# Who makes the low parts of the second and third super-block's operands: DVE or POOL

## The chip, the cores and the metric

The kernel runs on one core of one Trainium2 chip. The metric is the device time of one launch in microseconds. TensorE is called PE, VectorE DVE, ScalarE ACT, GpSimd POOL and SyncE SP.

## The reference

One layer of a streaming encoder with a width of 1024 runs over 2096 columns (2064 of a new stream and 32 of a running one). The mixer comes first, the SwiGLU feed-forward part second:

```python
xp = xp + mp                                   # mixer
xp = xp + _swiglu(_rmsnorm(xp, norm2_g[l]), w_gu[l], w_down[l])

def _swiglu(xn, w_gu, w_down):                 # w_gu 1024 x 5632, w_down 2816 x 1024
    gu = xn @ w_gu
    g, u = jnp.split(gu, [D_FF], axis=-1)
    return (jax.nn.silu(g) * u) @ w_down
```

A final RMSNorm gives the outputs. Everything is float32.

## The kernel before

**Precision.** Each float32 operand of a matmul is split in two fp32r tiles: a high part, which ACT writes as a copy, and a low part, the operand less its high part. Three matmuls (high by high, high by low, low by high) give one product. This is done to weights and to activations alike. DVE makes the low parts of the weights (`split_lo`, L1590), ACT their high parts (`split_hi`, L795), in a ring of three slots (`wring`).

**Feed-forward part.** The columns stand in three super-blocks s = 0, 1, 2 of 2 x 348, 2 x 346 and 2 x 346 columns. The two halves of a super-block and the two halves of the contraction and of the output make a 2 x 2 by 2 x 2 matrix product, which is done with seven products in place of eight. For each of four contraction tiles j the seven operands are four tiles as they are, and three differences with a fourth made of them. They stand in `ycomb[:, combination, high or low, j, :]`. A super-block runs through gate/up steps 0 to 10 (`gate_up`) and down groups 0 to 5 (`down`), in the order gu0, gu1, gu2, dn0, gu3, gu4, dn1, ... gu9, gu10, dn4, dn5. Each step and group uses seven weight slots. A slot is 24 matmuls in dn4 and 12 in dn5, where the group has one pair of tiles instead of two. Down products land in PSUM, and DVE adds them to `xacc` (`add_down`, L1579), 14 additions a group.

**The operand of the next super-block** is made while dn4 and dn5 run, by three engines:

- POOL, `operand(s, j)` (L550 to L561), for j = 0 to 3. It issues three DMAs that load four tiles of `ys` into `work`, waits for them, makes the differences of 692 columns (L557) and of 346 (L559 and L561). Loads of j = 2 and 3 first wait for the low parts of j - 2, the differences of j for the low parts of j - 1. POOL starts when DVE has made the last low part of gate/up step 10.
- ACT, `operand_hi(s, j)` (L1004 to L1009): four copies, the first two once the loads have landed, the third after L559, the fourth after L561. They are placed in ACT's list in group dn4 before the weight splits of slots 2, 3, 5 and 6 (`REBUILD`), each split being that for three slots later.
- DVE, `operand_lo(s, j)` (L1465 to L1471): four subtractions of 692, 346, 1038 and 346 columns, each after ACT's matching copy, placed in DVE's list in group dn4 after the additions of slots 2, 3, 5 and 6.

Each engine's list is in order, so a wait in it holds all that follows. PE's first matmul of the next super-block waits for all 16 high and 16 low increments:

```python
if p == k == 0:
    pe.wait_ge(a_hi, 16 * (s + 1))
    pe.wait_ge(a_lo, 16 * (s + 1))
```

The operand of super-block 0 is made in the mixer's last block by the same functions, at other places (`BUILD`, `TAKE`).

Of the kernel before, what the change touches and what calls it, by code (L numbers as in the profile page):

```python
# [31 lines left out]
NT = 3  # L32
TH = (348, 346, 346)
# [134 lines left out]
REBUILD = {2: 0, 3: 1, 5: 2, 6: 3}  # L168
# [64 lines left out]
def build(nc, dx, dwm, dws, dcst, dfix, dst0, graw, draw, dy, dst, fused, sgu, sdn, x1s, ys):  # L233
    f32 = mybir.dt.float32
# [3 lines left out]
    MUL, ADD, SUB = ALU.mult, ALU.add, ALU.subtract  # L238
    base = -(-nc.sbuf_base // 64) * 64
    ctx = ExitStack()  # L240
    with ctx:
        def sem(name):
            return ctx.enter_context(nc.semaphore(name))

        def at(offset, name, shape, dt=f32):
            return nc.alloc_sbuf_tensor_at(name, shape, dt, offset=base + offset)
# [10 lines left out]
        work = at(e0, "work", [P, 15, HW])  # L257
# [8 lines left out]
        ycomb = at(a0, "ycomb", [P, 7, 2, 4, HW], f32r)  # L266
# [22 lines left out]
        y_made, y_in, y_diff, a_hi, a_lo = sem("y_made"), [sem("y_in0"), sem("y_in1")], sem("y_diff"), sem("a_hi"), sem("a_lo")  # L289
# [95 lines left out]
        def after_gu(s, what, i):  # L385

            n = STEPS.index((what, i))
            return n > 0 and STEPS[n - 1][0] == "gu"
# [5 lines left out]
        def y_base(j):  # L394

            return 7 + 4 * (j % 2)
# [76 lines left out]
        def _(pool):  # L473
# [67 lines left out]
            def load_acc(s):  # L541
                for m in range(KT):
                    pool.dma_start(xacc[:, m, 0:2 * TH[s]], x1s[m, :, TO[s]:TO[s] + 2 * TH[s]]).then_inc(x1_in, 16)

            def operand(s, j):

                n, w, b0 = 4 * s + j, TH[s], y_base(j)
                if j >= 2:
                    pool.wait_ge(a_lo, 4 * (n - 1))
                pool.dma_start(work[:, b0:b0 + 2, 0:w],  # L550
                               ys[j, :, TO[s]:TO[s] + 2 * w].rearrange("p (t c) -> p t c", t=2)).then_inc(y_in[j % 2], 16)
                pool.dma_start(work[:, b0 + 2, 0:w], ys[j + 4, :, TO[s] + w:TO[s] + 2 * w]).then_inc(y_in[j % 2], 16)
                pool.dma_start(work[:, b0 + 3, 0:w], ys[j + 4, :, TO[s]:TO[s] + w]).then_inc(y_in[j % 2], 16)
                pool.wait_ge(y_in[j % 2], 48 * (n // 2 + 1))
                if j:
                    pool.wait_ge(a_lo, 4 * n)
                nc.gpsimd.tensor_tensor(work[:, 3:5, 0:w], work[:, b0 + 1:b0 + 3, 0:w], work[:, b0:b0 + 2, 0:w], SUB).then_inc(y_diff, 1)  # L557
                pool.wait_ge(y_diff, 3 * n + 1)
                nc.gpsimd.tensor_tensor(work[:, 5, 0:w], work[:, b0 + 2, 0:w], work[:, 3, 0:w], SUB).then_inc(y_diff, 1)  # L559
                pool.wait_ge(y_diff, 3 * n + 2)  # L560
                nc.gpsimd.tensor_tensor(work[:, 6, 0:w], work[:, b0 + 3, 0:w], work[:, 5, 0:w], SUB).then_inc(y_diff, 1)  # L561

            pool.wait_ge(tables_in, 32)
            for b in range(NB):
                chunks = prep_range(b)
# [35 lines left out]
            for s in range(NT - 1):  # L601
                pool.wait_ge(h_lo, 4 * PAIRS * (s + 1))
                pool.wait_ge(y_kept, 16 * KT * NB)
                for j in range(4):
                    operand(s + 1, j)
                for n, m in enumerate(NORM_ORDER):
                    pool.wait_ge(y_done, 8 * s + n + 1)
                    pool.dma_start(dy[m, :, TO[s]:TO[s] + 2 * TH[s]], xacc[:, m, 0:2 * TH[s]]).then_inc(y_stored, 16)
                pool.wait_ge(y_stored, 16 * KT * (s + 1))
                load_acc(s + 1)  # L610
# [609 lines left out]
        def _(dve):  # L1220
# [241 lines left out]
            def operand_lo(s, j):  # L1462
                n, w, b0 = 4 * s + j, TH[s], y_base(j)
                dve.wait_ge(a_hi, 4 * n + 1)
                V.tensor_tensor(ycomb[:, 0:2, 1, j, 0:w], work[:, b0:b0 + 3:2, 0:w], ycomb[:, 0:2, 0, j, 0:w].bitcast(f32), SUB).then_inc(a_lo, 1)  # L1465
                dve.wait_ge(a_hi, 4 * n + 2)
                V.tensor_tensor(ycomb[:, 5, 1, j, 0:w], work[:, b0 + 3, 0:w], ycomb[:, 5, 0, j, 0:w].bitcast(f32), SUB).then_inc(a_lo, 1)
                dve.wait_ge(a_hi, 4 * n + 3)
                V.tensor_tensor(ycomb[:, 2:5, 1, j, 0:w], work[:, 3:6, 0:w], ycomb[:, 2:5, 0, j, 0:w].bitcast(f32), SUB).then_inc(a_lo, 1)
                dve.wait_ge(a_hi, 4 * n + 4)  # L1470
                V.tensor_tensor(ycomb[:, 6, 1, j, 0:w], work[:, 6, 0:w], ycomb[:, 6, 0, j, 0:w].bitcast(f32), SUB).then_inc(a_lo, 1)  # L1471

            def norm_sum(s, i):
                n, w = KT * s + i, 2 * TH[s]
                dve.wait_ge(n_sq, n + 1)
                if i == 0:
                    V.tensor_copy(ntot[:, 0:w], nsq[:, n % 2, 0:w]).then_inc(n_sum, 1)
                else:
                    dve.wait_ge(n_sum, n)
                    V.tensor_tensor(ntot[:, 0:w], ntot[:, 0:w], nsq[:, n % 2, 0:w], ADD).then_inc(n_sum, 1)  # L1480
# [100 lines left out]
            def split_lo(n):  # L1581
                if n >= NS:
                    return
                dve.wait_ge(w_hi, n + 1)
                name, c = SLOTS[n], slot_width(n)
                if name[0] == "w":
                    V.scalar_tensor_tensor(wring[:, n % RING, 1, :], wraw[:, n % RAW, :], cst[:, PSC, name[2]:name[2] + 1],
                                           wring[:, n % RING, 0, :].bitcast(f32), MUL, SUB).then_inc(w_lo, 1)
                else:
                    V.tensor_tensor(wring[:, n % RING, 1, 0:c], wraw[:, n % RAW, 0:c], wring[:, n % RING, 0, 0:c].bitcast(f32), SUB).then_inc(w_lo, 1)  # L1590
# [136 lines left out]
            for s in range(NT):  # L1727
                for what, i in STEPS:
                    if what == "gu":
                        gate_up(s, i)  # L1730
                        continue
                    for hh in range(14):
                        if hh % 2 == 0 and (hh or not after_gu(s, "dn", i)):
                            split_lo(SLOT[("dn", s, i, hh // 2)] + RING - 1)
                        add_down(s, i, hh)
                        if hh % 2 and s < NT - 1 and i == 4 and hh // 2 in REBUILD:
                            operand_lo(s + 1, REBUILD[hh // 2])
                        if hh % 2 and s == NT - 1 and i == 5 and hh >= 9:
                            norm_sum(s, hh // 2 - 4)
            for i in range(3, KT):  # L1740
# [79 lines left out]
```

## Time and profile before

| what | value |
|---|---|
| time, median of 3 runs | 2899.11 us (2894.8 to 2900.23) |
| the profiled execution | 2899.26 us, span 2897.4 us |
| PE busy | 2720.9 us (94%) |
| DVE busy | 2104.6 us (73%) |
| ACT busy | 1367.3 us (47%) |
| POOL busy | 250.6 us (9%) |
| mean granted clock of TensorE | 0.981 |

The span is what the trace covers, the execution's own time is a little longer. Busy shares are averages over stages with different limits. The rows below are in microseconds from the start of the span, unless marked ns; what stands in square brackets is how long the engine idled before the instruction, and what ended that.

### The profile page before, as it was taken

The numbers are of one execution on the slowest core, as the hardware profiler recorded it, in microseconds if no ns is written. First come the engines' busy times: TensorE is split into PE (matmuls) and PEld (weight loads), VectorE is DVE, ScalarE is ACT, GpSimd is POOL, SyncE is SP. The second block draws the span as 40 slices with busy tenths as digits, with TensorE's granted clock in tenths as the row PEclk, the third lists the DMA queues.
The fourth block names the chain that finished last, engine by engine and source line by source line (L and its number), as shares of the span: only waits on it lengthen the run. The fifth ranks groups of instructions, "written<-read, shape, count | busy, mean of one in ns | idle before, by whom it ended". The sixth has DMA issues, their size and how long they took to land.

```text
span 2897.4 us, 39533 instructions
## 1 busy us (share of the span) xinstructions
PE 2720.9 (94%) x15404; PEld 2676.2 (92%) x15404; DVE 2104.6 (73%) x2784; ACT 1367.3 (47%) x1849; POOL 250.6 (9%) x425
## 2 busy tenths in 40 slices
PE   8999999999999999999799999889999979999995
PEld 6999999999999999999799999789999979899995
DVE  6867788688868877876676566787666677666667
ACT  6743583366447544833444343454344435334442
POOL 2000101020110011021300000300000030000000
PEclk9999999999999999999899999999999999999998
DMA  6353567456655855574543443445343434534442
GB/s 225 125 180 122 187 224 265 150 202 240 212 184 184 280 190 174 201 260 139 178 154 131 133 128 127 130 142 197 125 131 131 133 129 143 190 124 131 131 131 87
DMA packets 166729, 481.87 MB, mean 166 GB/s; under 512 B 18800, under 2 KB 41840, under 8 KB 166544
## 3 DMA queue, kind: packets, MB, share of 16 engines
q1 hardware_dynamic: 124368, 345.21, 35.7%
q0 software_dynamic: 31664, 117.66, 11.8%
q10 hardware_dynamic: 10512, 16.46, 2.0%
q8 instruction: 124, 2.03, 0.3%
q14 instruction: 61, 0.50, 0.1%
HBM read 414.75 MB, written 64.51 MB: 165 GB/s over the span
## 4 chain that ended last, share of the span: by engine, by line
PE 67%; DVE 15%; ACT 7%; issue 5%; DMA 2%; POOL 2%; SPq 0%; DVEq 0%; ACTq 0%; POOLq 0%
PE ps L635 67%; DVE wring L1590 2%; ACT wring L795 2%; DVE xacc L1579 1%; DMA work<-ys 1%; DVE tmp L1336 1%; DVE work L1545 1%; DVE gb L1305 1%; DVE tmp L1439 1%; POOL work L557 1%; ACT work L1056 1%; DVE main L1721 1%; DVE tmp L1252 1%; DVE xlo L1256 1%; ACT L896 1%
## 5 line engine op out<-in xcount | busy, mean ns | idle before, releaser
L1590 DVE TENSOR_TENSOR wring<-wraw,wring 128x1024 fp32r<-128x1024 f32 (+1 forms) x637 | 768.1, 1206 | 298.8 <-ACT wring L795 296.6
L795 ACT ACTIVATE wring<-wraw 128x1024 fp32r<-128x1024 f32 (+1 forms) x637 | 661.6, 1039 | 620.1 <-PE ps L635 616.6
L635 PE MATMUL ps<-ycomb,wring 128*128 128x346 f32 (+1 forms) x5544 | 890.7, 322 | 23.3 <-issue 14.0
L635 PEld LDWEIGHTS ps<-ycomb,wring 128*128 128x128 f32 x5544 | 887.3, 190 | 25.0 <-issue 25.0
L635 PE MATMUL ps<-xhi,wring 128*128 128x416 f32 (+1 forms) x2560 | 707.7, 354 | 32.9 <-DVE wring L1590 27.6
L635 PE MATMUL ps<-hcomb,wring 128*128 128x346 f32 (+1 forms) x2772 | 477.2, 333 | 90.9 <-DVE xacc L1579 65.8
L635 PEld LDWEIGHTS ps<-hcomb,wring 128*128 128x128 f32 x2772 | 461.3, 197 | 104.8 <-issue 82.4
L635 PEld LDWEIGHTS ps<-xhi,wring 128*128 128x128 f32 x2560 | 482.3, 188 | 47.3 <-DVE wring L1590 26.4
L635 PE MATMUL ps<-xlo,wring 128*128 128x416 f32 (+1 forms) x1280 | 451.5, 353 | 0.0
L635 PE MATMUL ps<-yhi,wring 128*128 128x416 f32 x1280 | 347.1, 351 | 2.6 <-DVE wring L1590 2.6
L1579 DVE TENSOR_TENSOR xacc<-ps,xacc 128x692 f32<-128x692 f32 (+1 forms) x252 | 218.3, 877 | 94.4 <-PE ps L635 90.8
L635 PEld LDWEIGHTS ps<-xlo,wring 128*128 128x128 f32 x1280 | 241.3, 189 | 3.9
L635 PEld LDWEIGHTS ps<-yhi,wring 128*128 128x128 f32 x1280 | 240.2, 188 | 4.8 <-DVE wring L1590 3.2
L635 PE MATMUL ps<-ylo,wring 128*128 128x416 f32 x640 | 224.5, 351 | 0.0
L635 PE MATMUL ps<-mhi,wring 128*128 128x416 f32 x640 | 173.0, 350 | 0.0
L1503 DVE TENSOR_TENSOR work<-ps,work 128x692 f32<-128x692 f32 (+1 forms) x99 | 87.1, 880 | 105.0 <-PE ps L635 105.0
L1015 ACT ACTIVATE work<-ps 128x692 f32<-128x692 f32 (+1 forms) x99 | 74.2, 749 | 177.1 <-PE ps L635 177.0
L635 PEld LDWEIGHTS ps<-ylo,wring 128*128 128x128 f32 x640 | 120.0, 188 | 1.4
L635 PEld LDWEIGHTS ps<-mhi,wring 128*128 128x128 f32 x640 | 120.0, 188 | 0.2
L635 PE MATMUL ps<-mlo,wring 128*128 128x416 f32 x320 | 111.8, 350 | 0.0
L1305 DVE SCALAR_TENSOR_TENSOR gb<-tbuf,cst,gb 128x416 f32<-128x416 f32 (+3 forms) x144 | 80.3, 581 | 20.7 <-ACT gb L864 12.8
L1056 ACT ACTIVATE work<-work 128x1038 f32<-128x1038 f32 (+1 forms) x33 | 35.4, 1074 | 114.9 <-DVE work L1503 114.9
(209 smaller groups left out, 2231.7 us busy)
## 6 DMA issues: line engine op xcount, KB each, us to landing
wraw<-dwm SPq DMA_DIRECT2D x247, 512.0 KB, 3.5
wraw<-sgu SPq DMA_DIRECT2D x132, 512.0 KB, 3.2
wraw<-graw SPq DMA_DIRECT2D x99, 512.0 KB, 3.4
wraw<-sdn SPq DMA_DIRECT2D x120, 256.0 KB, 2.8
wraw<-draw SPq DMA_DIRECT2D x90, 256.0 KB, 2.9
pbuf<-graw POOLq DMA_DIRECT2D x22, 1024.0 KB, 6.9
sgu<-pbuf POOLq DMA_DIRECT2D x22, 1024.0 KB, 6.2
wraw<-fused SPq DMA_DIRECT2D x40, 512.0 KB, 3.3
```

What stands on the lines that cost most here:

```text
L557: nc.gpsimd.tensor_tensor(work[:, 3:5, 0:w], work[:, b0 + 1:b0 + 3, 0:w], work[:, b0:b0 + 2, 0:w], SUB).then_inc(y_diff, 1)
L635: mm = nc.tensor.matmul(out, wt[:, c * P:(c + 1) * P], x, start=(first and q == 0), stop=(last and q == 2), skip_group_check=chain)
L795: A(wring[:, n % RING, 0, 0:c], wraw[:, n % RAW, 0:c], ACT.Copy, scale=cst[:, PSC, name[2]:name[2] + 1] if name[0] == "w" else 1.0).then_i ...
L896: A(tmp[:, 4 * j + 2, 0:bw], tmp[:, 4 * j, 0:bw], ACT.Exp, scale=lac[:, 0, h:h + 1]).then_inc(a_done, 1)
L1015: A(work[:, first:first + 8:7, 0:TH[s]], both(name, TH[s]), ACT.Copy).then_inc(cleared[BANK[name] // 2], 1)
L1056: A(work[:, 0:3, 0:w], work[:, 0:3, 0:w], ACT.Silu).then_inc(silu3, 1)
L1252: V.tensor_tensor(tmp[:, 4 + k % 2, 0:LW], xring[:, k % XR, :], rstd[1][:, 0:LW], MUL).then_inc(xr_done, 1)
L1256: V.scalar_tensor_tensor(xlo[:, m, 0:LW], tmp[:, 4 + m % 2, 0:LW], cst[:, G1, m:m + 1], xhi[:, m, 0:LW].bitcast(f32), MUL, SUB).then_inc(x ...
L1305: V.scalar_tensor_tensor(gb[:, h, c:c + n], t[:, o + v:o + v + n], cst[:, CW0 + v, h:h + 1], gb[:, h, c:c + n], MUL, ADD).then_inc(tap, 1)
L1503: V.tensor_tensor(c, both(name, TH[s]), c, ADD).then_inc(cleared[BANK[name] // 2], 1)
L1579: V.tensor_tensor(out, both(name, w), out, ADD).then_inc(cleared[BANK[name] // 2], 1)
L1590: V.tensor_tensor(wring[:, n % RING, 1, 0:c], wraw[:, n % RAW, 0:c], wring[:, n % RING, 0, 0:c].bitcast(f32), SUB).then_inc(w_lo, 1)
```

## The change

POOL gets a function `operand_rest(s, j)` with the same four subtractions and waits as `operand_lo`, and calls it directly behind `operand(s + 1, j)` for super-blocks 1 and 2. DVE's calls in the down groups go. DVE's `operand_lo(0, ...)` for super-block 0 stays.

```diff
+            def operand_rest(s, j):
+                n, w, b0 = 4 * s + j, TH[s], y_base(j)
+                pool.wait_ge(a_hi, 4 * n + 1)
+                nc.gpsimd.tensor_tensor(ycomb[:, 0:2, 1, j, 0:w], work[:, b0:b0 + 3:2, 0:w], ycomb[:, 0:2, 0, j, 0:w].bitcast(f32), SUB).then_inc(a_lo, 1)
+                pool.wait_ge(a_hi, 4 * n + 2)
+                nc.gpsimd.tensor_tensor(ycomb[:, 5, 1, j, 0:w], work[:, b0 + 3, 0:w], ycomb[:, 5, 0, j, 0:w].bitcast(f32), SUB).then_inc(a_lo, 1)
+                pool.wait_ge(a_hi, 4 * n + 3)
+                nc.gpsimd.tensor_tensor(ycomb[:, 2:5, 1, j, 0:w], work[:, 3:6, 0:w], ycomb[:, 2:5, 0, j, 0:w].bitcast(f32), SUB).then_inc(a_lo, 1)
+                pool.wait_ge(a_hi, 4 * n + 4)
+                nc.gpsimd.tensor_tensor(ycomb[:, 6, 1, j, 0:w], work[:, 6, 0:w], ycomb[:, 6, 0, j, 0:w].bitcast(f32), SUB).then_inc(a_lo, 1)
...
                 for j in range(4):
                     operand(s + 1, j)
+                    operand_rest(s + 1, j)
...
                         add_down(s, i, hh)
-                        if hh % 2 and s < NT - 1 and i == 4 and hh // 2 in REBUILD:
-                            operand_lo(s + 1, REBUILD[hh // 2])
```

## Rows read from the trace of the kernel before

**Rows 1.** The page's first line.

```profile
span 2897.4 us, 39533 instructions
```

**Rows 2.** Stretch, length, PE, PEld, DVE, ACT, POOL busy (count), granted clock, DMA share, GB/s.

```profile
1845.91:1902.02 56.11, 41.62 (x229) 39.30 (x229) 46.10 (x56) 19.78 (x28) 24.30 (x24) 0.91 0.43 139
2336.02:2392.56 56.54, 43.23 (x229) 41.12 (x230) 45.87 (x56) 19.86 (x28) 24.16 (x24) 0.88 0.43 138
```

**Rows 3.** Waits, 1820 to 1890 us: engine, line, released by: total, times, longest.

```profile
PE ps L635 <- DVE xacc L1579: 14.6, 6, 5.0
...
ACT ycomb L1007 <- POOL work L559: 8.6, 4, 2.9
```

**Rows 4.** POOL in order of time, first stretch, and one row of the second.

```profile
1845.91 0.73 POOL L550 DMA_DIRECT2D work<-ys  x1 [365.62 <-DVE hcomb L1565]
...
1847.29 0.54 POOL L553 DMA_DIRECT2D work<-ys  x1
1850.97 1.69 POOL L557 TENSOR_TENSOR work<-work 128x692 f32<-128x692 f32 x1 [3.15 <-DMA work<-ys]
1852.75 1.79 POOL L559 TENSOR_TENSOR work<-work 128x346 f32<-128x346 f32 x1
1854.62 0.94 POOL L561 TENSOR_TENSOR work<-work 128x346 f32<-128x346 f32 x1
1855.49 0.73 POOL L550 DMA_DIRECT2D work<-ys  x1
...
1877.95 1.98 POOL L557 TENSOR_TENSOR work<-work 128x692 f32<-128x692 f32 x1 [2.90 <-DMA work<-ys]
1880.01 1.97 POOL L559 TENSOR_TENSOR work<-work 128x346 f32<-128x346 f32 x1
...
2370.88 1.53 POOL L559 TENSOR_TENSOR work<-work 128x346 f32<-128x346 f32 x1
```

**Rows 5.** PE in order of time, first stretch, and one row of the second.

```profile
1886.32 5.56 PE L635 MATMUL ps<-hcomb,wring 128*128 128x348 f32 x24 [5.00 <-DVE xacc L1579]
1892.43 4.41 PE L635 MATMUL ps<-hcomb,wring 128*128 128x348 f32 x24 [0.55 <-DVE xacc L1579]
...
1902.02 26.80 PE L635 MATMUL ps<-ycomb,wring 128*128 128x346 f32 x168
...
2392.56 26.82 PE L635 MATMUL ps<-ycomb,wring 128*128 128x346 f32 x168
```

**Rows 6.** DVE's groups, 1845.9 to 1902 us: count, busy us, mean ns, idle before.

```profile
L1469 DVE TENSOR_TENSOR ycomb<-work,ycomb 128x1038 fp32r<-128x1038 f32 x4 | 4.9, 1236 | 2.7 <-ACT ycomb L1007 2.7
...
L1465 DVE TENSOR_TENSOR ycomb<-work,ycomb 128x692 fp32r<-128x692 f32 x4 | 4.4, 1093 | 0.2 <-ACT ycomb L1004 0.2
L1467 DVE TENSOR_TENSOR ycomb<-work,ycomb 128x346 fp32r<-128x346 f32 x4 | 2.8, 698 | 0.0
L1471 DVE TENSOR_TENSOR ycomb<-work,ycomb 128x346 fp32r<-128x346 f32 x4 | 2.1, 513 | 0.0
```

**Rows 7.** POOL's groups of differences, 1840 to 1890 us.

```profile
L557 POOL TENSOR_TENSOR work<-work 128x692 f32<-128x692 f32 x4 | 7.2, 1796 | 12.0 <-DMA work<-ys 12.0
L559 POOL TENSOR_TENSOR work<-work 128x346 f32<-128x346 f32 x4 | 6.1, 1534 | 0.3
L561 POOL TENSOR_TENSOR work<-work 128x346 f32<-128x346 f32 x4 | 3.9, 968 | 0.3
```

**Rows 8.** Two weight splits in DVE's order of time.

```profile
1851.71 2.04 DVE L1590 TENSOR_TENSOR wring<-wraw,wring 128x1024 fp32r<-128x1024 f32 x1 [0.27 <-ACT wring L795]
...
1858.22 1.21 DVE L1590 TENSOR_TENSOR wring<-wraw,wring 128x1024 fp32r<-128x1024 f32 x1
```

**Rows 9.** ACT in order of time, behind the fourth operand's third copy.

```profile
1883.00 0.49 ACT L1009 ACTIVATE ycomb<-work 128x346 fp32r<-128x346 f32 x1
1883.40 1.13 ACT L795 ACTIVATE wring<-wraw 128x512 fp32r<-128x512 f32 x2
```

**Rows 10.** Busy time and granted clock as PE comes back.

```profile
1886.00:1888.00 2.00, 1.69 (x6) 1.72 (x7) 1.56 (x3) 0.00 (x0) 0.00 (x0) 0.50 0.41 131
```

## The prediction

> **What bounds the kernel now.** I read the span first: 2897.4 us [rows 1], with 1.86 us outside it in the profiled execution's own 2899.26 us. The code then says where the changed work runs: between the last low part of gate/up step 10 (the DVE increment that opens POOL's operand work) and the first matmul of the next super-block. It happens twice, so I asked for the busy time of each engine in those two stretches [rows 2]. They are 56.11 and 56.54 us long; PE is busy in 41.62 and 43.23 us of them and POOL in 24.30 and 24.16 us. The reader is to see that neither is full: here something waits on something in turn, and a share of busy time says nothing of what ends the stretch.
>
> The waits of the first stretch [rows 3] show PE held by DVE's additions to xacc for 14.6 us, and ACT held by POOL's second difference (L559) for 8.6 us. These belong together. DVE is late because the operand's low part stands ahead of the next addition in its list and waits for ACT's high part; ACT is late because its high part waits for POOL's differences, and the next weight split stands behind it. So I followed POOL in order of time [rows 4]. One operand is a strictly serial turn: three DMA issues from 1845.91 to 1847.83, the wait for their landing until 1850.97, three differences until 1855.56, and at 1855.49 the next operand's issues. POOL never loads ahead, since the loads stand behind the differences of the operand before. Four turns bring the fourth operand's L559 to its end at 1880.01 + 1.97 = 1881.98, 36.07 us after the start. In the second stretch it ends at 2370.88 + 1.53 = 2372.41 [rows 4], 36.39 us after 2336.02 [rows 2]. From there to the next super-block's first matmul it takes 1902.02 - 1881.98 = 20.04 us and 2392.56 - 2372.41 = 20.15 us [rows 4, 5]. That is the sum to be changed: 36.1 + 20.0 = 56.1 us.
>
> **The change, part by part.** It *removes* four low-part subtractions per operand from DVE, four operands in each of two stretches. In the first stretch the four groups take 4.4 + 2.8 + 4.9 + 2.1 = 14.2 us [rows 6]. The same operand's first building, for super-block 0, stays on DVE.
>
> It *adds* four subtractions per operand to POOL, each behind ACT's matching high part, and they stand ahead of the next operand's three DMA issues. That last point is the heart of it: the whole price of one operand's low parts, R, is put before the next operand's load. POOL's trace has no operation on 1038 columns and none that writes fp32r, so R is bounded by its two other shapes. POOL's 692 columns take 1.80 us as a mean, its 346 columns 1.53 (L559) and 0.97 us (L561) [rows 7]; the least loaded single ones are 1.69 and 0.94 us [rows 4]. Between the latter two, 346 more columns cost 0.75 us, so 1038 cost an estimated 2.45 us. Central: 1.80 (692) + 1.25 (346, the mean of the two lines) + 2.45 (1038) + 0.97 (346), and four gaps of 0.07 us as between L557's end at 1852.66 and L559's start at 1852.75 [rows 4], give R = 6.75 us. Low end: 1.69 + 0.94 + 2.45 + 0.94 + 0.28 = 6.3 us. High end: with each of the four as slow as its worst neighbour (1.98, 1.97 [rows 4], 1038 at 2.45 + 1.03 = 3.5, 1.97, 0.28), 9.7 us. I take 6.75, nearer the low end, because those slow ones coincide with DVE work that now partly goes away. That ACT's part is awaited costs nothing more: POOL's first two low parts need only the copies that ACT makes during the differences, and the third needs the copy of the three differences, behind which L1009 starts at 1883.00, 1.0 us after the end of L559 [rows 9]; L561 and the first two low parts, 4 us together, hide it. If ACT came late to its high parts, that cover would be gone and POOL's turn would lengthen by as much; but ACT was the one that waited, 8.6 us [rows 3].
>
> The fourth operand's high part waits for three such R: +20.3 us (18.9 to 29.1).
>
> What comes back, first: POOL's differences run less disturbed. The twelve in the stretch take 7.2 + 6.1 + 3.9 = 17.2 us [rows 7]; at 1.69 and 0.94 us each they would take 14.3, so 2.9 us is the most. DVE loses 14.2 of some 46 busy us [rows 2, 6], a third, so I take a third: -1.0 us (-2.9 to 0). A DVE split of 1024 columns took 2.04 us during L557 and 1.21 us outside any POOL operation [rows 8], so both sides pay when they meet. The Trainium skill, page "SBUF — State Buffer", section "Who interferes with whom", says that a VectorE instruction with two SBUF inputs and a GpSimd instruction that reads SBUF exclude each other for the whole instruction; by that rule the new POOL subtractions collide with the splits but not with the xacc additions, whose one input is in PSUM. The trace agrees as far as this pair of durations shows it.
>
> Second, the tail behind the fourth L559. Before, ACT ended its high parts at 1883.49, 1.51 us after L559; the DVE low parts and one split more let PE restart at 1886.32, 4.34 us after it [rows 5, 9]. From there on PE had six weight slots of the last down group to do, twelve matmuls each (a row of 24 is two slots), until 1902.02: two slots until 1892.43 took 6.1 us, the other four 9.6, or 2.4 each [rows 5]. After, the longer waits leave PE time to do one of the six before the fourth operand is ready, since its weights are split ahead of that high part. Restart: 1.5 (ACT) + 0.6 (split [rows 9]) + 0.3 (gap [rows 8]) + 0.7 (DVE's split of 512 columns, somewhat over half of the 1.21 for 1024) = 3.1 us, and 1.1 for a collision of that DVE split with POOL's last low parts, which now run just then (0.8 us seen [rows 8], and somewhat more for a POOL operation of 2.45 us) = 4.2 us. Five slots: 6.1 + 3 x 2.4 = 13.3. Tail 17.5 us in place of 20.0: -2.5 us (-3.6 to +0.5). The first two slots are dear because of the clock: TensorE's granted clock was 0.50 of full speed (1.2 of 2.4 GHz) as PE came back after idling 5 us [rows 5, 10]. It will idle longer now, some 7, 7 and 13 us before three restarts, since ahead of the second, third and fourth operand the splits let it do only three, two and one slots of a 16 us turn (dn5's slots are half as long as dn4's); the first two restarts lie in time that POOL sets anyway, and the third is priced in the 6.1, with one more slot at the low clock (+1.3 us) as the upper end.
>
> The fourth operand's own low parts end 1.0 + 6.75 = 7.8 us after L559, 10 us before PE needs them; if that cover went they would delay directly. POOL's next duty is the store of finished outputs and the reload of xacc, tens of microseconds later, so nothing queued behind it notices. SP's queue is not passed by anything, and its weight loads are held by the splits, not the other way.
>
> Sum per stretch: +20.3 - 1.0 - 2.5 = +16.8 us, so the stretch grows from 56.1 to about 72.9. Two stretches: +33.6. The profiled 2899.26 becomes 2932.9, and since that execution stands 0.15 us above the median of 2899.11, the forecast is 2932 us (+1.1%).
>
> **The rivals.** *A, POOL's low parts cheaper than that, or partly hidden.* With R = 6.3, the full 2.9 us of relief and a tail shorter by 3.6: 18.9 - 2.9 - 3.6 = 12.4 per stretch, 2924 us; if PE's clock stays up besides (saving some 2 us) and the three-tile operation is 1 us cheaper than the line through the two shapes, 7.4 per stretch, 2914 us. For it: L559 and L561 fall to 0.94 us when undisturbed. Against it: L559's mean is 1.53 us. The Trainium skill, page "GPSIMD Engine Reference", section "Elementwise — side-by-side cycle accounting", gives about 2.6 cycles per element for a two-input operation at 1.2 GHz. An estimate from that page is 5.2 us for seven tiles of 346 columns without any overhead, and the sum by it would be about 2925 us, at the edge of this case; the 0.75 us that 346 more columns cost here is the same slope.
>
> *B, the exclusion bites.* R = 9.7, no relief, tail +0.5: 29.6 per stretch, 2958 us; halfway, 2945. For it: 2.04 against 1.21 us, and L559's mean of 1.53. Against it: in the long waits DVE has little left to do.
>
> *C, DVE's list is what ends the stretch, and the change makes it faster.* PE's largest wait names DVE (14.6 us [rows 3]), and DVE loses 14.2 us of work. If R were nothing, the relief and the shorter tail would give 3.5 us a stretch, 2892 us. The point from which this decides: 3R below 3.5, R below 1.2 us for seven tiles. The cheapest one-tile row alone is 0.94 us, so I give it almost nothing.
>
> *D, hidden anyway.* POOL is idle 31.8 us of the 56.1 [rows 2], and four R are 27 us, so by shares it fits: 2899 us. Against it: those idle times are waits for the loads of the same turn, which move back with it. It would need the loads to go out before the low parts, which the code doesn't do.
>
> **How the numbers follow.** Forecast case (2925 to 2941) 0.60; A (below 2925) 0.17; B (above 2941) 0.17; C 0.03; D 0.03. The range leaves out C, D and the far ends of A and B: 2915 to 2950 us. A measurement of this kernel tells no change from one within 0.2%, 5.8 us. Slower by more than that is the forecast with A and B, 0.94; the same 0.03; faster 0.03.
>
> **What the profile of the changed kernel would show.** The two stretches about 73 us long. POOL's turns 16 us in place of 9, with low parts of about 1.8, 1.25, 2.5 and 1 us, and the fourth L559 ending some 55 us after the start. ACT waiting long for the landing of the second to fourth operand, PE idle three times, 7, 7 and 13 us, with the clock at half after each. PE's waits named after DVE's wring splits and no longer after xacc. The stretches outside unchanged. The prediction is wrong if the POOL subtraction of three tiles is far from 2.5 us, if PE's idle time lasts past the restart for another reason, or if the fourth L559 moves by something other than three R.

## The result and the profile after

The changed kernel takes 2938.14 us (median of 4 runs, 2934.64 to 2941.59), the kernel before 2899.4 us (2894.8 to 2900.23) beside it. The ratio is 1.0137, with a 95% interval of 1.0119 to 1.0154: slower by 1.4%, 38.7 us by the medians. The profiled execution of the changed kernel took 2934.64 us, its lowest run; line numbers above 561 have moved (xacc L1591, splits L1602 and L807, PE L647, ACT's copies L1016 to L1021). The first lines of its page (PE's busy time rose by 6.7 us, from 2720.9):

```profile
span 2932.8 us, 39533 instructions
...
PE 2727.6 (93%) x15404; PEld 2682.7 (91%) x15404; DVE 2086.1 (71%) x2752; ACT 1366.3 (47%) x1849; POOL 299.9 (10%) x457
```

The same two stretches as in [rows 2], busy time by engine:

```profile
1844.71:1918.33 73.62, 45.00 (x229) 42.49 (x229) 36.99 (x40) 19.54 (x28) 48.88 (x40) 0.77 0.33 106
2352.89:2426.91 74.02, 43.85 (x229) 41.53 (x229) 36.84 (x40) 19.53 (x28) 48.80 (x40) 0.77 0.33 106
```

They grew by 73.62 - 56.11 = 17.5 us and 74.02 - 56.54 = 17.5 us. Together that is 35.0 of the 35.4 us by which the span grew (2932.8 against 2897.4), so all but 0.4 us of the loss lies there. POOL's busy time doubled in them, and every other engine's share fell.

POOL in order of time, the first stretch, its first turn and the fourth operand's first two differences (compare [rows 4]):

```profile
1844.71 0.73 POOL L550 DMA_DIRECT2D work<-ys  x1 [362.57 <-DVE hcomb L1577]
...
1849.97 1.68 POOL L557 TENSOR_TENSOR work<-work 128x692 f32<-128x692 f32 x1 [3.35 <-DMA work<-ys]
1851.73 0.94 POOL L559 TENSOR_TENSOR work<-work 128x346 f32<-128x346 f32 x1
...
1854.50 1.70 POOL L566 TENSOR_TENSOR ycomb<-work,ycomb 128x692 fp32r<-128x692 f32 x1
1856.16 1.92 POOL L568 TENSOR_TENSOR ycomb<-work,ycomb 128x346 fp32r<-128x346 f32 x1
1858.04 2.45 POOL L570 TENSOR_TENSOR ycomb<-work,ycomb 128x1038 fp32r<-128x1038 f32 x1
1860.44 0.95 POOL L572 TENSOR_TENSOR ycomb<-work,ycomb 128x346 fp32r<-128x346 f32 x1
1861.31 0.73 POOL L550 DMA_DIRECT2D work<-ys  x1
...
1895.71 1.65 POOL L557 TENSOR_TENSOR work<-work 128x692 f32<-128x692 f32 x1 [2.69 <-DMA work<-ys]
1897.44 0.91 POOL L559 TENSOR_TENSOR work<-work 128x346 f32<-128x346 f32 x1
```

One turn now goes from 1844.71 to 1861.31, 16.6 us, where it took 9.6: the four low parts L566 to L572 stand between the differences and the next load. The first of them starts at 1854.50 and the next load at 1861.31, so the low parts of the first operand cost 6.81 us; those of the second and third cost 7.21 and 6.15 us by the same reading. The fourth L559 ends at 1897.44 + 0.91 = 1898.35, 53.64 us after the start, and from there to the next super-block's first matmul it takes 19.98 us.

POOL's low parts by line (compare the differences in [rows 7]):

```profile
L570 POOL TENSOR_TENSOR ycomb<-work,ycomb 128x1038 fp32r<-128x1038 f32 x4 | 9.7, 2419 | 0.0
...
L566 POOL TENSOR_TENSOR ycomb<-work,ycomb 128x692 fp32r<-128x692 f32 x4 | 6.6, 1662 | 0.0
L568 POOL TENSOR_TENSOR ycomb<-work,ycomb 128x346 fp32r<-128x346 f32 x4 | 6.6, 1647 | 0.0
L572 POOL TENSOR_TENSOR ycomb<-work,ycomb 128x346 fp32r<-128x346 f32 x4 | 4.6, 1150 | 0.0
```

PE in order of time, the first stretch (compare [rows 5]):

```profile
1845.23 17.34 PE L647 MATMUL ps<-hcomb,wring 128*128 128x348 f32 x96 [2.34 <-DVE xacc L1591]
1873.25 11.63 PE L647 MATMUL ps<-hcomb,wring 128*128 128x348 f32 x54 [10.68 <-DVE xacc L1591]
1888.98 1.53 PE L647 MATMUL ps<-hcomb,wring 128*128 128x348 f32 x6 [4.10 <-DVE xacc L1591]
1902.46 6.09 PE L647 MATMUL ps<-hcomb,wring 128*128 128x348 f32 x24 [11.94 <-DVE xacc L1591]
1908.73 4.42 PE L647 MATMUL ps<-hcomb,wring 128*128 128x348 f32 x24 [0.19 <-DVE xacc L1591]
1913.35 3.10 PE L647 MATMUL ps<-hcomb,wring 128*128 128x348 f32 x18 [0.20 <-DVE xacc L1591]
1917.29 1.20 PE L647 MATMUL ps<-hcomb,wring 128*128 128x348 f32 x6 [0.85 <-DVE xacc L1591]
1918.33 26.80 PE L647 MATMUL ps<-ycomb,wring 128*128 128x346 f32 x168
```

PE idles three times for long, 10.7, 4.1 and 11.9 us. Behind the third it still has 24 + 24 + 18 + 6 matmuls to do, six slots, exactly as before. The longest waits from 1845 to 1920 us (total, times, longest):

```profile
PE ps L647 <- DVE xacc L1591: 30.3, 7, 11.9
ACT ycomb L1016 <- DMA work<-ys: 29.3, 3, 9.9
DVE wring L1602 <- ACT wring L807: 29.2, 6, 11.6
PEld ps L647 <- DVE wring L1602: 23.3, 2, 12.4
```

ACT stands at the landing of the next operand's loads for 29.3 us; DVE stands at a weight split that ACT hasn't made; PE's matmuls stand at DVE's additions and its weight loads (PEld) at DVE's splits.

### The profile page after: what moved, and what is told of

Its sections match the earlier page's. It is cut to its first block, busy times and chain, and to the rows that moved or that the text cites. A ratio compares the mean times of both kernels' runs of the same rounds, so it can differ in the third digit from the quotient of the medians.

```text
span 2932.8 us, 39533 instructions
## 1 busy us (share of the span) xinstructions
PE 2727.6 (93%) x15404; PEld 2682.7 (91%) x15404; DVE 2086.1 (71%) x2752; ACT 1366.3 (47%) x1849; POOL 299.9 (10%) x457
## 4 chain that ended last, share of the span: by engine, by line
PE 67%; DVE 15%; ACT 7%; issue 5%; POOL 4%; DMA 2%; SPq 0%; DVEq 0%; ACTq 0%; POOLq 0%
PE ps L647 66%; DVE wring L1602 2%; ACT wring L807 2%; DMA work<-ys 1%; DVE xacc L1591 1%; DVE tmp L1348 1%; DVE work L1557 1%; POOL work L557 1%; DVE gb L1317 1%; ACT work L1068 1%; DVE tmp L1451 1%; DVE main L1733 1%; DVE tmp L1264 1%; DVE xlo L1268 1%; ACT L908 1%
## 5 line engine op out<-in xcount | busy, mean ns | idle before, releaser
L1602 DVE TENSOR_TENSOR wring<-wraw,wring 128x1024 fp32r<-128x1024 f32 (+1 forms) x637 | 775.3, 1218 | 360.7 <-ACT wring L807 358.5
L807 ACT ACTIVATE wring<-wraw 128x1024 fp32r<-128x1024 f32 (+1 forms) x637 | 661.4, 1039 | 616.3 <-PE ps L647 616.2
L647 PE MATMUL ps<-ycomb,wring 128*128 128x346 f32 (+1 forms) x5544 | 893.6, 323 | 23.3 <-issue 13.7
L647 PEld LDWEIGHTS ps<-ycomb,wring 128*128 128x128 f32 x5544 | 890.4, 190 | 24.7 <-issue 24.7
L647 PE MATMUL ps<-xhi,wring 128*128 128x416 f32 (+1 forms) x2560 | 708.9, 354 | 32.5 <-DVE wring L1602 27.2
L647 PE MATMUL ps<-hcomb,wring 128*128 128x346 f32 (+1 forms) x2772 | 479.6, 334 | 119.7 <-DVE xacc L1591 94.1
L647 PEld LDWEIGHTS ps<-hcomb,wring 128*128 128x128 f32 x2772 | 463.2, 198 | 134.2 <-issue 87.8
L647 PEld LDWEIGHTS ps<-xhi,wring 128*128 128x128 f32 x2560 | 483.2, 189 | 46.8 <-DVE wring L1602 25.8
L647 PE MATMUL ps<-xlo,wring 128*128 128x416 f32 (+1 forms) x1280 | 452.1, 353 | 0.0
L647 PE MATMUL ps<-yhi,wring 128*128 128x416 f32 x1280 | 347.1, 351 | 2.6 <-DVE wring L1602 2.6
L1591 DVE TENSOR_TENSOR xacc<-ps,xacc 128x692 f32<-128x692 f32 (+1 forms) x252 | 218.5, 876 | 88.8 <-PE ps L647 86.7
L647 PEld LDWEIGHTS ps<-xlo,wring 128*128 128x128 f32 x1280 | 241.8, 189 | 3.9
L647 PEld LDWEIGHTS ps<-yhi,wring 128*128 128x128 f32 x1280 | 240.2, 188 | 4.8 <-DVE wring L1602 3.3
L647 PE MATMUL ps<-ylo,wring 128*128 128x416 f32 x640 | 224.5, 351 | 0.0
L647 PE MATMUL ps<-mhi,wring 128*128 128x416 f32 x640 | 173.0, 350 | 0.0
L647 PEld LDWEIGHTS ps<-ylo,wring 128*128 128x128 f32 x640 | 120.0, 188 | 1.4
L647 PEld LDWEIGHTS ps<-mhi,wring 128*128 128x128 f32 x640 | 120.0, 188 | 0.2
L647 PE MATMUL ps<-mlo,wring 128*128 128x416 f32 x320 | 111.8, 350 | 0.0
L1068 ACT ACTIVATE work<-work 128x1038 f32<-128x1038 f32 (+1 forms) x33 | 35.5, 1074 | 114.9 <-DVE work L1515 114.9
```

The source lines that it names most:

```text
L647: mm = nc.tensor.matmul(out, wt[:, c * P:(c + 1) * P], x, start=(first and q == 0), stop=(last and q == 2), skip_group_check=chain)
L807: A(wring[:, n % RING, 0, 0:c], wraw[:, n % RAW, 0:c], ACT.Copy, scale=cst[:, PSC, name[2]:name[2] + 1] if name[0] == "w" else 1.0).then_i ...
L1068: A(work[:, 0:3, 0:w], work[:, 0:3, 0:w], ACT.Silu).then_inc(silu3, 1)
L1591: V.tensor_tensor(out, both(name, w), out, ADD).then_inc(cleared[BANK[name] // 2], 1)
```

## The experiments

For each run the trace gives the same two numbers per stretch, counted here from the end of gate/up step 10's last low part (0.3 to 0.4 us ahead of POOL's first issue): when the fourth operand's second difference ends, and the tail from there to the next super-block's first matmul. Each ratio is to executions of the kernel before that were taken beside that run (their medians go from 2898.15 to 2900.86 us), so rows are better compared by ratio than by time. The four rows behind changed start from the changed kernel, the last six from the kernel before; last_operand is the kernel before with one operand's low parts on POOL.

| kernel | time, us | ratio to before, 95% | fourth difference, us | tail, us |
|---|---|---|---|---|
| before | 2899.4 | | 36.5, 36.7 | 20.0, 20.2 |
| changed | 2938.14 | 1.0137 (1.0119 to 1.0154) | 54.1, 54.4 | 20.0, 20.0 |
| load_ahead | 2922.97 | 1.0076 (1.0061 to 1.0091) | 46.3, 46.3 | 20.0, 20.3 |
| twice | 2950.88 | 1.0174 (1.0159 to 1.0189) | 61.8, 62.0 | 20.3, 20.6 |
| adds_first | 2941.23 | 1.0134 (1.0117 to 1.0151) | 55.9, 57.2 | 20.1, 20.0 |
| adds_first_both | 2937.07 | 1.0130 (1.0112 to 1.0149) | 55.0, 57.4 | 17.5, 16.8 |
| last_operand | 2901.02 | 1.0001 (0.9989 to 1.0014) | 36.2, 35.5 | 20.4, 20.3 |
| before_loads_ahead | 2901.57 | 1.0002 (0.9993 to 1.0011) | 37.4, 37.7 | 20.2, 19.9 |
| first_load_early | 2900.18 | 1.0000 (0.9991 to 1.0010) | 37.2, 35.8 | 20.2, 20.6 |
| two_loads_early | 2898.99 | 0.9997 (0.9987 to 1.0007) | 36.8, 36.6 | 20.2, 20.2 |
| before_adds_first | 2901.53 | 1.0010 (1.0000 to 1.0020) | 36.7, 36.4 | 19.6, 19.5 |
| loads_by_act | 2894.69 | 0.9987 (0.9979 to 0.9996) | 33.6, 35.8 | 20.2, 19.5 |
| one_slot_earlier | 2892.34 | 0.9982 (0.9971 to 0.9992) | 32.6, 34.1 | 21.0, 20.9 |

### The order of loads on POOL

```diff
+                operand_load(s + 1, 0)
                 for j in range(4):
-                    operand(s + 1, j)
+                    operand_diff(s + 1, j)
+                    if j < 3:
+                        operand_load(s + 1, j + 1)
                     operand_rest(s + 1, j)
```

> The changed kernel, but POOL issues the next operand's three loads between the differences and the low parts of the present one. Theory (POOL's serial turn sets the stretch): a turn is then differences 3.7 + issues 1.8 + low parts 6.7 = 12.2 us in place of some 15.3, so the fourth L559 ends some 44 us after the start of the stretch in place of 53.6, both stretches shrink by 9 to 10 us, and the time falls by about 19 us to 2919 us, still 20 us above the kernel before. Rival (POOL's and DVE's exclusion at SBUF, or DVE's list, sets it): the order of loads changes nothing, 2938 us.

It took 2922.97 us, 15.2 less than the changed kernel by the medians. POOL, from the second operand's issues to its differences:

```profile
1858.64 0.73 POOL L553 DMA_DIRECT2D work<-ys  x1
...
1860.47 2.73 POOL L572 TENSOR_TENSOR ycomb<-work,ycomb 128x692 fp32r<-128x692 f32 x1
...
1866.48 0.90 POOL L578 TENSOR_TENSOR ycomb<-work,ycomb 128x346 fp32r<-128x346 f32 x1
1867.52 1.64 POOL L563 TENSOR_TENSOR work<-work 128x692 f32<-128x692 f32 x1
```

The differences follow the low parts at once, with no wait for the landing between. The turns are 13.4, 12.9 and 11.8 us, longer than the 12.2 expected mainly because the first low part took 2.7 us in two of them, and the fourth difference ends at 46.3 in place of 54.1 us. Both stretches shrink by 7.7 us. So some two fifths of the change's loss (15.2 of 38.7 us) come from the landing standing in series with the low parts; the rest is put down to POOL's own work in the turn. The rival, that order doesn't matter, fell.

### Twice the largest low part

```diff
                 pool.wait_ge(a_hi, 4 * n + 3)
+                nc.gpsimd.tensor_tensor(ycomb[:, 2:5, 1, j, 0:w], ...).then_inc(y_twice, 1)
+                pool.wait_ge(y_twice, n - 3)
                 nc.gpsimd.tensor_tensor(ycomb[:, 2:5, 1, j, 0:w], ...).then_inc(a_lo, 1)
```

> The changed kernel with POOL's three-tile subtraction (L570, 2.42 us) done twice. Theory: whatever is put before the next operand's loads counts three times a stretch, so 3 x 2.5 x 2 = +15 us on the changed kernel, 2953 us. Rival (only part of POOL's time is on the path, the rest of the loss comes from collisions with DVE): less than half of that.

It took 2950.88 us, 12.7 more than the changed kernel by the medians; the spans of the two profiled executions differ by 2947.6 - 2932.8 = 14.8 us. The expected 15 us and the rival's bound of half of that lie on either side of 12.7, which is much nearer the first. The fourth difference moved by 7.7 us, three times 2.6, where the added operation takes 2.4. So an addition to POOL's turn counts fully and three times.

### The last operand alone

```diff
                 for j in range(4):
                     operand(s + 1, j)
-                    operand_rest(s + 1, j)
+                    if j == 3:
+                        operand_rest(s + 1, j)
```

DVE keeps the low parts of the other three.

> POOL makes the low parts of the fourth operand alone, DVE those of the other three as before. Theory (the price is what stands ahead of the next loads): behind the fourth nothing waits, its 6.7 us end some 10 us before PE needs them, so this part of the change costs nothing: 2899 us, or 1 to 3 us less as DVE's restart is some 1 us earlier. Rival (collisions of POOL's subtractions with DVE's splits are what costs): a quarter of the loss, +9 us, 2909 us.

It took 2901.02 us, ratio 1.0001 (0.9989 to 1.0014): no change, and the rival's +9 us, 0.3%, lies outside the interval. POOL, the fourth operand in the first stretch:

```profile
1879.94 0.93 POOL L559 TENSOR_TENSOR work<-work 128x346 f32<-128x346 f32 x1
...
1881.82 1.66 POOL L566 TENSOR_TENSOR ycomb<-work,ycomb 128x692 fp32r<-128x692 f32 x1
...
1887.13 1.38 POOL L572 TENSOR_TENSOR ycomb<-work,ycomb 128x346 fp32r<-128x346 f32 x1
```

Those low parts end at 1887.13 + 1.38 = 1888.51, and the next super-block's first matmul starts 12.7 us later, at 1901.25. This is the third part of the same statement: behind the fourth operand no load waits, and no price can be seen.

### Additions ahead of splits

```diff
+                        late = s < NT - 1 and i == 4
-                        if hh % 2 == 0 and (hh or not after_gu(s, "dn", i)):
+                        if not late and hh % 2 == 0 and (hh or not after_gu(s, "dn", i)):
                             split_lo(SLOT[("dn", s, i, hh // 2)] + RING - 1)
                         add_down(s, i, hh)
+                        if late and hh % 2 and hh > 1:
+                            split_lo(SLOT[("dn", s, i, hh // 2)] + RING - 1)
```

> The changed kernel, but in group dn4 DVE does a slot's two additions to xacc before the low part of the weights two slots on, in place of after it. Theory: the additions are held by a split that waits for ACT, so PE stands one slot earlier than its weights would let it; with the order turned, PE has one slot of the last group done when the fourth operand is ready, the tail behind the fourth L559 falls from 20.0 to about 17.5 us, and the time by about 5 us to 2933. Rival: the tail is set by the restart itself (clock, splits), and the time stays at 2938. In both the fourth L559 keeps its 53.6 us.

It took 2941.23 us, at a ratio of 1.0134 no different from the changed kernel, and the tail stayed at 20.0 to 20.1: the expectation fell, for a reason that the trace shows. PE and, below, DVE's splits of this kernel in the first stretch:

```profile
1874.19 8.29 PE L647 MATMUL ps<-hcomb,wring 128*128 128x348 f32 x36 [7.29 <-DVE wring L1602]
1904.64 8.54 PE L647 MATMUL ps<-hcomb,wring 128*128 128x348 f32 x36 [22.15 <-DVE xacc L1591]
```

```profile
1888.21 1.08 DVE L1602 TENSOR_TENSOR wring<-wraw,wring 128x512 fp32r<-128x512 f32 x1 [7.07 <-ACT wring L807]
1902.60 1.10 DVE L1602 TENSOR_TENSOR wring<-wraw,wring 128x512 fp32r<-128x512 f32 x1 [13.31 <-ACT wring L807]
```

PE does 36 matmuls from 1874.19, the last slot of dn4 and the first of dn5, and then idles 22.15 us, though the split of the next slot is ready at 1889.29. DVE has taken the next split, which belongs to dn5 where the order wasn't turned, and waits 13.31 us at it with the additions of PE's last slot behind. So I turned the order there too (`late = s < NT - 1 and i >= 4`, and the split of dn5's first slot after its additions).

> The changed kernel, with DVE's additions ahead of its splits in dn4 and in dn5. In the run that turned them in dn4 alone, PE did slots 6 and 7 early and then idled 22 us with the weights of slot 8 ready, since DVE stood at dn5's first split before the additions of slot 7. Theory: with dn5 turned as well, PE has slot 8 done too when the fourth operand is ready, and only five slots are left: the tail falls from 20.0 to some 17.5 us, and the time from that of the changed kernel by 0 to 5 us (in the other run POOL's turns grew by 2 us a stretch through collisions with the splits). Rival (the restart alone sets the tail): tail 20 us.

PE in the first stretch:

```profile
1873.07 8.53 PE L647 MATMUL ps<-hcomb,wring 128*128 128x348 f32 x36 [7.13 <-DVE wring L1602]
1888.81 3.82 PE L647 MATMUL ps<-hcomb,wring 128*128 128x348 f32 x12 [7.21 <-DVE xacc L1591]
1903.06 8.95 PE L647 MATMUL ps<-hcomb,wring 128*128 128x348 f32 x36 [10.43 <-DVE xacc L1591]
1912.20 4.40 PE L647 MATMUL ps<-hcomb,wring 128*128 128x348 f32 x24 [0.20 <-DVE xacc L1591]
1916.45 5.82 PE L647 MATMUL ps<-ycomb,wring 128*128 128x346 f32 x35
```

PE now does one more slot (12 matmuls at 1888.81) ahead of the fourth operand, and 36 + 24 behind it, five slots: the tail is 17.5 and 16.8 us. The time is 2937.07 us, since the fourth differences ended 1 to 3 us later than in the changed kernel; the first differences of the second operand started at 22.7 and 24.7 us in place of 21.7 and 21.5. In the first stretch the first operand's low parts met DVE's splits at other places than in the changed kernel: the first took 2.70 us and the last 1.93, in place of 1.70 and 0.95. In the second stretch the last took 1.92 us, and the wait for the second operand's landing was 4.8 us in place of 2.9. The ratio, 1.0130 (1.0112 to 1.0149), can't be told from the changed kernel's: what the tail gave, the longer turns took back for the most part.

### What bounds the kernel before

```diff
+                operand_load(s + 1, 0)
+                operand_load(s + 1, 1)
+                operand_diff(s + 1, 0)
-                for j in range(4):
-                    operand(s + 1, j)
+                for j in range(1, 4):
+                    if j < 3:
+                        operand_load(s + 1, j + 1)
+                    operand_diff(s + 1, j)
```

> The kernel before, low parts on DVE, but in the second and third super-block's building POOL issues the loads of the second operand at once behind those of the first, and those of the third and fourth one operand ahead of their differences. Theory (the serial turn sets the end in the kernel before too): a turn is issues 1.8 + L557 and L559 3.3 + ACT's copy 1.1 + DVE's low parts 1.8, some 8 us in place of 9.2 at worst and 7 at best, so the fourth L559 ends 4 to 6 us earlier in each stretch and the time falls by 8 to 12 us, to 2887 to 2891. Rival (DVE's list, or the ring of weights, ends the stretch): 2899 as before.

2901.57 us, no difference: my theory, that POOL's serial turn sets the end in the kernel before as well, fell in this form. The fourth operand no longer waited for its landing but for DVE's low parts. Its first differences in this run, and below them the same instruction in the second stretch of the kernel before:

```profile
1881.03 1.98 POOL L563 TENSOR_TENSOR work<-work 128x692 f32<-128x692 f32 x1 [5.36 <-DVE ycomb L1482]
```

```profile
2368.82 1.97 POOL L557 TENSOR_TENSOR work<-work 128x692 f32<-128x692 f32 x1 [2.91 <-DVE ycomb L1471]
```

With the load ahead POOL waited 5.36 us for DVE's last low part of the third operand; in the kernel before it had been released by the same low part, though in its other seven turns the landing came last.

In the next two the first operand's loads use the four free tile rows (`y_base` swapped for super-blocks 1 and 2) and go out before the wait on step 10.

```diff
+                pool.wait_ge(a_lo, 16 * (s + 1))
+                pool.wait_ge(y_kept, 16 * KT * NB)
+                operand_load(s + 1, 0)
                 pool.wait_ge(h_lo, 4 * PAIRS * (s + 1))
-                for j in range(4):
+                operand_diff(s + 1, 0)
+                for j in range(1, 4):
                     operand(s + 1, j)
```

> The kernel before, low parts on DVE, but the first operand's loads go to the tile rows that gate/up step 10 doesn't use, so POOL issues them before it waits for that step's last low part. In the trace of before the landing costs 5.1 us after the start of the stretch. If POOL's turn alone sets the end, both stretches lose 5 us and the time falls to 2889 us. If, as the run with loads ahead suggests, the kernel before is held as much by the place of DVE's low parts behind the additions of slot 2 (they end 12.8 us after the start), the second operand's differences start 2 us earlier at best: 2895 us. If DVE's list alone sets it: 2899 us.

In the second of the two the second operand's loads stand ahead of the first operand's differences as well:

```diff
                 pool.wait_ge(h_lo, 4 * PAIRS * (s + 1))
+                operand_load(s + 1, 1)
                 operand_diff(s + 1, 0)
+                operand_diff(s + 1, 1)
-                for j in range(1, 4):
+                for j in (2, 3):
                     operand(s + 1, j)
```

> As the run with the first load early, and the second operand's loads issued before the first operand's differences, so that the second operand's differences wait for DVE's low parts alone (12.8 us after the start, in place of 14.9). Theory (DVE's place in its list sets the first two operands, POOL's turn the last two): the same as the run with the first load early or at most 2 us a stretch less, 2891 to 2895 us. If POOL's turn alone sets the end: 10 us a stretch less than before, 2880 us.

2900.18 and 2898.99 us: no difference either. POOL in the run with the first load early:

```profile
1843.96 1.65 POOL L563 TENSOR_TENSOR work<-work 128x692 f32<-128x692 f32 x1 [357.04 <-DVE hcomb L1574]
1845.69 1.79 POOL L565 TENSOR_TENSOR work<-work 128x346 f32<-128x346 f32 x1
...
1858.12 2.50 POOL L563 TENSOR_TENSOR work<-work 128x692 f32<-128x692 f32 x1 [7.87 <-DVE ycomb L1480]
```

The first operand's second difference ends at 3.6 us in place of 9.0, but the second operand's differences start at 14.2 in place of 14.9, released by DVE's fourth low part of the first operand. DVE makes that behind the additions of slot 2, and those wait for PE. I read from these waits that POOL's turn and DVE's place in its list are two limits of nearly equal length, so that taking one away shows nothing. That reading is argued from the releasers, not shown by a time.

The last three are meant to take both away, step by step. The first of them turns additions and splits in dn4 and dn5, as in adds_first_both.

> The kernel before, with DVE's additions ahead of its weight splits in dn4 and dn5, low parts behind both. On the changed kernel this shortened the tail from 20.0 to 17.5 and 16.8 us, but POOL's turns grew by 1 to 3 us a stretch. If the tail is as general here: 2.5 us less per stretch, 2894 us; if the turns grow as they did there, 2897 to 2900 us. If DVE's low parts, not its splits, hold PE in this kernel: no change of the tail, 2899 us.

2901.53 us, ratio 1.0010 (1.0000 to 1.0020), tails 19.6 and 19.5. The tail gained only 0.4 to 0.7 us: PE's restart waits for additions that stand behind DVE's low parts of the fourth operand in the list. The second adds early loads, and issues the third's and fourth's from ACT's queue:

```diff
                 A(ycomb[:, 2:5, 0, j, 0:w], work[:, 3:6, 0:w], ACT.Copy).then_inc(a_hi, 1)
+                if s and 1 <= j <= 2:
+                    c0, b1 = j + 1, y_base(s, j + 1)
+                    act.wait_ge(a_lo, 4 * n)
+                    act.dma_start(work[:, b1:b1 + 2, 0:w], ...).then_inc(y_act[c0 % 2], 16)
+                    act.dma_start(work[:, b1 + 2, 0:w], ...).then_inc(y_act[c0 % 2], 16)
+                    act.dma_start(work[:, b1 + 3, 0:w], ...).then_inc(y_act[c0 % 2], 16)
```

> As before_adds_first, and the first operand's loads go out early, the second's at the start of the stretch, the third's and fourth's on ACT's queue behind ACT's third copy of the operand ahead of them. Theory (in the kernel before POOL's serial turns and DVE's place in its list each set half of the stretch, so both must go): the third and fourth operand's differences wait for DVE's low parts alone, turns of 7 to 8 us in place of 9, the fourth L559 ends 3 to 5 us earlier, tail 17.5 to 20: 2885 to 2893 us. Rival (something else ends the stretch, such as the ring of weights): as before_adds_first.

2894.69 us, ratio 0.9987 (0.9979 to 0.9996), so the rival, the same as before_adds_first, fell. The third moves the building one slot ahead (`REBUILD = {1: 0, 2: 1, 4: 2, 5: 3}`).

> As loads_by_act, and the four operands are made one slot of dn4 earlier (slots 1, 2, 4, 5) in ACT's and DVE's lists. Theory: DVE's low parts of the first operand then end some 9 us after the start of the stretch in place of 12.8, all turns follow 4 us earlier, and one more slot of PE's work is left behind them, which costs back 2 to 4: 2880 to 2890 us. If PE's slots rather than the operand's turns set the end, the same as loads_by_act or up to 4 us slower.

2892.34 us, ratio 0.9982 (0.9971 to 0.9992): the lowest median, 0.2% below the kernel before, though its interval overlaps that of loads_by_act. Both gained less than expected. In one_slot_earlier the fourth difference came 4 and 3 us earlier than in the kernel before, and the tail grew by 1, as more of PE's work stands behind it. One reason for the small gain is in the traces: ACT issues the third operand's loads behind its third copy, which waits for POOL's second difference, and that operand's own differences still waited 3.0 to 3.5 us for the landing in both runs. So POOL's turn was shortened and not taken away. What each of the combined edits gives alone is not shown.

## Why the prediction was right, and where its terms were not

The forecast was 2932 us with a range of 2915 to 2950, slower at 0.94; measured were 2938.14. The mechanism, the place and the sign were right, and three runs show them: a doubled low part counts three times, loads put ahead take back 15 us, and the fourth operand's low parts cost nothing. By its own steps:

- **The price R of one operand's low parts.** 6.75 us forecast; 6.81, 7.21 and 6.15 measured, 20.2 for three against 20.3. The extrapolated three-tile operation took 2.42 us against 2.45. The four lines came out as 1.66, 1.65, 2.42 and 1.15 us against 1.80, 1.25, 2.45 and 0.97. Part of the agreement is luck: the two operations of 346 columns were 0.4 and 0.2 us dearer than forecast through collisions with DVE, and the 0.28 us for four gaps was not there. (By its rows the gap between L557 and L559 is 0.09 us, not 0.07; POOL's low parts start 0.03 to 0.05 us before the recorded end of the instruction ahead.)
- **Relief of the differences.** -1.0 us forecast, -2.6 measured: the fourth L559 moved by 53.64 - 36.07 = 17.6 us where three low parts cost 20.2. The term was mis-sized. The twelve differences take 6.7 + 3.7 + 4.6 = 15.0 us now, 2.2 less than the 17.2 before; the rest is mostly shorter waits for the landing (11.7 us in place of 12.0). I scaled the term by DVE's lost busy time, but behind the first turn DVE stands idle at a split while POOL makes the differences, and only one difference still met a split (L561 in the first turn, 1.79 us).
- **The tail.** -2.5 us forecast, none measured (19.98 against 20.04). This step failed: "the longer waits leave PE time to do one of the six before the fourth operand is ready". The weights were ready, but DVE stood at a later split with the additions behind it, and PE can't go on without those. When the additions were put first in both groups, PE did that slot, and the tails were 17.5 and 16.8 us, so the arithmetic was right and its assumption wrong. The restart itself came 1902.46 - 1898.35 = 4.1 us after L559, against 4.2 forecast; it is the sixth slot that made the difference. The expected collision at the restart is there (a split of 512 columns took 2.20 us, below), but it fell on the split after the one that PE waited for.
- **The sum.** +16.8 a stretch forecast, +17.5 measured. That it is so close is luck: the relief was 1.6 us too small and the tail 2.5 us too short, and these two errors have opposite signs. Two stretches give 35.0 of the profiled execution's 35.4 us. The medians differ by 38.7 us; the profiled execution of the changed kernel was the lowest of its four, and a median of so few leaves the remaining 3 us open.
- **PE's idle times** came out as 10.7, 4.1 and 11.9 us in place of 7, 7 and 13, and the waits of PE's matmuls stayed named after xacc (30.3 us) instead of the splits, for the same reason as the tail. The waits of its weight loads are named after the splits (23.3 us), as forecast.
- **The rivals.** R was 6.7 us as a mean and not 6.3 or less, so cheaper low parts (A) fell. The exclusion (B) is real but small: the four low parts of 346 columns that ran longer in the first three turns (1.92, 1.94, 1.36 and 1.37 us, against 0.93 alone) hold 2.9 of the 20.2 us. DVE's list as the sole limit (C) fell, and hidden (D) too: by shares POOL had room, in turns it had not. Of the kernel before, the prediction took POOL's serial turn for what sets the end; the runs with loads ahead and loads early show that shortening it alone gains nothing, so DVE's low parts hold the stretch about as long. That error didn't reach the sum, since in the changed kernel POOL makes the low parts itself and its turn of 16 us is the longer one by far.

The granted clock behaved as priced. Busy time and granted clock (the third number from the end) as PE came back from its third idling:

```profile
1902.00:1904.00 2.00, 1.54 (x5) 1.57 (x6) 2.00 (x3) 0.00 (x0) 2.00 (x2) 0.50 0.41 131
1904.00:1906.00 2.00, 2.00 (x8) 1.82 (x7) 2.00 (x2) 0.00 (x0) 2.00 (x2) 0.50 0.00 0
1906.00:1908.00 2.00, 2.00 (x11) 1.87 (x11) 1.70 (x4) 0.63 (x1) 0.00 (x0) 0.82 0.42 131
1908.00:1910.00 2.00, 1.81 (x12) 1.56 (x11) 2.00 (x4) 0.63 (x1) 0.00 (x0) 1.00 0.60 176
```

The clock is 0.50 of full speed (1.2 of 2.4 GHz) in the rows from 1902 to 1906, 0.82 in the next and full from 1908 on, though PE had idled 12 us and not 5 as in [rows 10]; the first two slots took 1908.73 - 1902.46 = 6.3 us against 6.1.

## What to carry to other kernels

Before moving work to an engine with a low busy share, write down that engine's turn and see whether the new work stands between one item's result and the next item's load: there it counted once per item here, at a busy share of 9%, and only the last item was free. If it must stand there, put the next load ahead of it, which took back two fifths of the loss here. Where taking away one limit changes nothing, look for a second of equal length; here going after both gained 0.2%. In a list in order, an instruction that waits for something late holds PE if it stands ahead of one that frees PE; turning the two shortened the changed kernel's tail by some 3 us a stretch, but POOL's turns grew by nearly as much, through collisions among other things, so look at what the turned order will run beside.

## What the runs showed of the hardware

A subtraction on DVE and one on POOL, each with both inputs in SBUF, shut each other out for whole instructions, in either direction. Changed kernel, first DVE's splits, then POOL's low parts at the same time:

```profile
1871.09 1.22 DVE L1602 TENSOR_TENSOR wring<-wraw,wring 128x1024 fp32r<-128x1024 f32 x1 [11.41 <-ACT wring L807]
...
1873.81 2.21 DVE L1602 TENSOR_TENSOR wring<-wraw,wring 128x512 fp32r<-128x512 f32 x1
...
1903.02 2.20 DVE L1602 TENSOR_TENSOR wring<-wraw,wring 128x512 fp32r<-128x512 f32 x1
```

```profile
1871.15 1.94 POOL L568 TENSOR_TENSOR ycomb<-work,ycomb 128x346 fp32r<-128x346 f32 x1
1873.05 2.42 POOL L570 TENSOR_TENSOR ycomb<-work,ycomb 128x1038 fp32r<-128x1038 f32 x1
```

POOL's subtraction of 346 columns starts 0.06 us after DVE's split at 1871.09 and takes 1.94 us, where others of its shape take 0.91 to 0.95: the split ended at 1872.31, and POOL needed 0.78 us more. Then DVE's split of 512 columns starts at 1873.81 within POOL's three-tile subtraction, which ends at 1875.47, and ends 0.55 us later, after 2.21 us, where 0.68 is its time alone. POOL was not slowed in that case. The Trainium skill, page "SBUF — State Buffer", section "Who interferes with whom", has this as an exclusive lock, and the durations agree. DVE's additions to xacc, one input of which is in PSUM, were not held: the one at 1858.80 took its usual 0.88 us in the middle of POOL's L570 (1858.04 to 1860.49).

Of the four low parts on POOL the first and the third keep their time (1.66 and 2.42 us). The second bears a collision in all four turns (1.92, 1.94, 1.36, 1.36 us), since DVE's split, like the low parts, follows ACT's copies; the fourth bears one in the second and fourth turn (1.37 us each, against 0.95 and 0.91).
